# The heads loop of a gated delta rule: gate read from PSUM, a mask added by TensorE, partial sums left to TensorE, a product moved by a round, filling matmuls

## The reference, cut to what matters

```python
decay = jnp.exp(jnp.where(lower, g[..., :, None] - g[..., None, :], -jnp.inf))
L = jnp.where(strict, jnp.einsum('bhncd,bhnsd->bhncs', kb, k) * decay, 0.0)
T = lax.linalg.triangular_solve(eye + L, ...)
u = T @ vb
w = T @ (kb * jnp.exp(g)[..., None])
attn = jnp.einsum('bhncd,bhnsd->bhncs', q, k) * decay
...
    v_new = u_n - jnp.einsum('bhcd,bhde->bhce', w_n, state)
    o = q_n @ state + a_n @ v_new
...
zg = jax.nn.silu(z)
o = rmsnorm(o, norm_w) * zg
return o @ w_out
```

## Time and profile before

| | |
|---|---|
| runs | 1623.2 us median of 3 (1621.7 to 1625.29) |
| profiled execution | 1621.4 us, with a span of 1619.6 us |
| TensorE busy | 1554.8 us (96%) |
| VectorE, ScalarE, GpSimd busy | 1109.9, 932.7 and 493.4 us |
| granted TensorE clock, mean | 0.987 |
| heads loop, first p0 to last d5 | 196.3 to 327.1 us |

### The profile page before, as it was taken

How to read it: one execution, slowest core, us unless ns; L and a number is a source line. 1 busy time by engine, 2 the same in 40 slices (tenths; PEclk the granted TensorE clock), 3 DMA queues, 4 the chain that set the end, 5 groups by cost and what they waited for, 6 DMA issues and landing times.

```text
span 1619.6 us, 37025 instructions
## 1 busy us (share of the span) xinstructions
PE 1554.8 (96%) x13269; PEld 1429.3 (88%) x13269; DVE 1109.9 (69%) x2304; ACT 932.7 (58%) x1763; POOL 493.4 (30%) x405
## 2 busy tenths in 40 slices
PE   7899999899999999999999999999999999999998
PEld 6899877798998899888999999999999888888886
DVE  3787768656556653776478888798888555555554
ACT  1766567744555555545354444799898544555554
POOL 4000278661000040000067777766565100000000
PEclk9999979899999999999999999999999999999999
DMA  9668412454443344247455555544444666666663
GB/s 295 219 184 278 150 55 82 133 163 130 151 131 118 111 156 131 79 157 156 104 150 167 168 168 172 162 143 135 140 131 143 182 194 194 193 192 190 194 193 127
DMA packets 211832, 255.89 MB, mean 158 GB/s; under 512 B 15912, under 2 KB 193804, under 8 KB 211724
## 3 DMA queue, kind: packets, MB, share of 16 engines
q1 hardware_dynamic: 211723, 254.39, 53.2%
HBM read 253.29 MB, written 1.05 MB: 157 GB/s over the span
## 4 chain that ended last, share of the span: by engine, by line
PE 72%; DVE 11%; issue 5%; DMA 4%; ACT 4%; SPq 2%; DVEq 0%; ACTq 0%
PE ps L2253 22%; PE ps L2861 22%; PE ps L2843 10%; PE ps L2831 3%; DMA raw<-in_u_experts 3%; PE ps L2273 2%; PE ps L2551 2%; DVE raw L2014 2%; SPq L580 2%; PE ps L2628 1%; DVE w_lo L1396 1%; PE ps L2451 1%; DMA arena<-in_ada_w 1%; DVE arena L2067 1%; PE ps L2648 1%
## 5 line engine op out<-in xcount | busy, mean ns | idle before, releaser
L742 POOL TENSOR_TENSOR w_lo<-raw,w_hi 128x1024 fp32r<-128x1024 f32 x128 | 307.6, 2406 | 337.7 <-ACT w_hi L1265 337.6
L2253 PE MATMUL ps<-x_hi,w_hi 128*128 128x256 f32 x1088 | 315.3, 290 | 8.3 <-DVE w_lo L1396 3.0
L2253 PE MATMUL ps<-x_hi,w_lo 128*128 128x256 f32 x1088 | 308.2, 283 | 0.0
L2253 PE MATMUL ps<-x_lo,w_hi 128*128 128x256 f32 x1088 | 308.2, 283 | 0.0
L2212 DVE TENSOR_TENSOR w_lo<-raw,w_hi 128x1024 fp32r<-128x1024 f32 x124 | 152.0, 1226 | 143.2 <-ACT w_hi L1374 143.2
L1374 ACT ACTIVATE w_hi<-raw 128x1024 fp32r<-128x1024 f32 x124 | 131.6, 1061 | 168.0 <-PE ps L2861 168.0
L2253 PEld LDWEIGHTS ps<-x_hi,w_hi 128*128 128x128 f32 x1088 | 209.1, 192 | 15.3 <-issue 6.0
L2253 PEld LDWEIGHTS ps<-x_lo,w_hi 128*128 128x128 f32 x1088 | 209.2, 192 | 1.3 <-issue 1.2
L2253 PEld LDWEIGHTS ps<-x_hi,w_lo 128*128 128x128 f32 x1088 | 209.0, 192 | 0.0
L1265 ACT ACTIVATE w_hi<-raw 128x1024 fp32r<-128x1024 f32 x128 | 134.9, 1054 | 113.4 <-DVE raw L2014 113.2
L2806 PE MATMUL ps<-x_hi,w_hi 128*128 128x256 f32 x576 | 166.3, 289 | 10.6 <-ACT arena L1287 9.7
(11 more groups left out here) (446 smaller groups left out, 3563.7 us busy)
## 6 DMA issues: line engine op xcount, KB each, us to landing
raw<-in_u_experts SPq DMA_DIRECT2D x512, 128.0 KB, 2.7
raw<-in_v_experts SPq DMA_DIRECT2D x128, 512.0 KB, 4.3
arena<-in_ada_w SPq DMA_DIRECT2D x18, 1024.0 KB, 7.8
raw<-in_a_w_in SPq DMA_DIRECT2D x12, 1024.0 KB, 5.7
arena<-in_a_w_in SPq DMA_DIRECT2D x12, 1024.0 KB, 5.7
raw<-in_b_w_in SPq DMA_DIRECT2D x8, 1024.0 KB, 5.7
arena<-in_b_w_in SPq DMA_DIRECT2D x8, 1024.0 KB, 5.6
raw<-in_w_in SPq DMA_DIRECT2D x8, 1024.0 KB, 5.6
```

Source lines behind the costliest of these rows:

```text
L742: pool.tensor_tensor(UTL[e], UT[e % 2], UTH[e].bitcast(F32), ALU.subtract).then_inc(utl_ready, 1)
L2253: ins = mm(o[:, b * S:b * S + S], w[:, slot, kk, b * P:b * P + P], xx[:, (kk + turn) % KC, :], start=(kk == 0 and n == 0), stop=(kk == k - ...
```

## The change

- `decays` is gone from VectorE. A new `setup_masks` on TensorE adds `negu` (now bf16) to ROWS in PSUM, by two matmuls with a bf16 identity for each of two heads, after `betas` has read ROWS. `setup_decays` reads its exponent from PSUM, and `setup_values` waits for it.
- `finish_out` loses its copy to OS. A new `gated` on VectorE multiplies A2, read from PSUM, with the norm weight and the gate, into ZB, behind m4. F5 waits for it too, since it writes the same bank. `normed` is left with one instruction for each head.
- GpSimd leaves out the last of its 7 additions. `modulator` takes four matmuls in place of two, two for each of its 128-column halves, and stands behind F1 of the next round.
- `keep_wide` issues filling matmuls (bf16, 512 columns, result unused). A middle round has two in front of d0 and one in front of d4; rounds 0 and 7 have more.
- The orders change: `setup_keys` stands behind d1, F2 behind p2, `norm_sums` in front of p5, `betas` in front of c2, `lowers` behind m3, `setup_v` ahead of `spread`, and in round 7 the splits of ZB (L1405) one step earlier.

```diff
-                for half, done in ((4, 8), (2, 12), (1, 14)):
+                for half, done in ((4, 8), (2, 12)):
...
             def setup_decays(r):
+                if r.at:
+                    act.wait_ge(h_kd, r.count(2))
+                    act.wait_ge(h_at, r.count(2))
+                    act.wait_ge(h_lt, r.count(2))
                 for g in range(2):
                     act.wait_ge(h_dta, r.nth(g))
                     for cc in range(2):
-                        act.activation(two(DT[g])[:, cc, :], two(DT[g])[:, cc, :], ACT.Exp,
+                        act.activation(two(DT[g])[:, cc, :], ROWS[g][:, cc * 128:cc * 128 + 128], ACT.Exp,
...
-            def finish_out(r):
+            def finish_squares(r):
+                for g in range(2):
+                    act.wait_ge(h_o, r.nth(g))
+                    act.activation(SQo[g], A2[g], ACT.Square).then_inc(h_sq, 1)
...
                 if f:
-                    finish_out(f)
+                    finish_squares(f)
+                if n:
+                    setup_v(n)
                 spread(i, 0)
                 spread(i, 1)
-                if n:
-                    setup_v(n)
                 spread(i, 2)
...
-            def decays(r):
-                if r.at:
-                    v.wait_ge(h_kd, r.count(2))
-                    v.wait_ge(h_at, r.count(2))
-                for g in range(2):
-                    v.wait_ge(h_eg, r.nth(g))
-                    v.tensor_tensor(two(DT[g]), two(ROWS[g][:, 0:256]), bcast(negu, 2), ALU.add).then_inc(h_dta, 1)
...
-            def normed(r, g):
+            def gated(r):
+                if r.at >= 6:
+                    v.wait_ge(z_late, 1)
+                for g in range(2):
+                    v.wait_ge(h_sq, r.nth(g))
+                    zb = ZB[:, r.heads[g], :]
+                    v.scalar_tensor_tensor(zb, A2[g], COLS[:, CAN:CAN + 1], zb, ALU.mult, ALU.mult).then_inc(h_os, 1)
+
+            def normed(r, g):
                 v.wait_ge(h_orn, r.nth(g))
                 v.wait_ge(h_os, r.nth(g))
-                v.scalar_tensor_tensor(OS[g], OS[g], COLS[:, CAN:CAN + 1], RNo[g], ALU.mult, ALU.mult).then_inc(h_og, 1)
-                v.wait_ge(h_og, r.nth(g, 1, 1, 2))
                 zb = ZB[:, r.heads[g], :]
-                v.tensor_tensor(zb, OS[g], zb, ALU.mult).then_inc(h_out, 1)
+                v.tensor_tensor(zb, zb, RNo[g], ALU.mult).then_inc(h_out, 1)
...
-            def setup_values(r):
+            def setup_masks(r):
                 for g in range(2):
                     pe.wait_ge(h_eg, r.nth(g))
                     pe.wait_ge(h_xm, r.nth(g))
+                    for cc in range(2):
+                        ins = mm(ROWS[g][:, cc * 128:cc * 128 + 128], ident16, negu, start=False, stop=True, skip_group_check=True)
+                    ins.then_inc(h_dta, 1)
+
+            def setup_values(r):
+                for g in range(2):
+                    pe.wait_ge(h_dt, r.nth(g, 2))
...
                 for cc in range(2):
-                    ins = mm(MODP[:, cc:cc + 1], RAW[MOD_SLOT[r.side]][:, 0, cc * 128:cc * 128 + 128], ones[:, 0:1], start=True, stop=True)
+                    for half in range(2):
+                        ins = mm(MODP[:, cc:cc + 1], RAW[MOD_SLOT[r.side]][:, half, cc * 128:cc * 128 + 128], ones[:, 0:1],
+                                 start=(half == 0), stop=(half == 1))
...
+            def keep_wide(bank_, n):
+                for _ in range(n):
+                    mm(bank_[:, :], ident16, BG3, start=True, stop=True)
...
             def inner(i, f, n):
                 level_p(i, 0)
-                level_d(i, 0)
+                level_d(i, 0, 2)
                 if f:
                     finish(f, 0)
-                level_p(i, 1)
+                level_p(i, 1, 0 if f else 2)
                 if f:
                     finish(f, 1)
+                    modulator(f)
+                level_d(i, 1, 0 if f else 2)
                 if n:
                     setup_keys(n)
-                level_d(i, 1)
+                level_p(i, 2, 0 if n else 1)
                 if f:
                     finish(f, 2)
-                level_p(i, 2)
                 if n:
                     setup_rows(n)
-                level_d(i, 2)
+                level_d(i, 2, 0 if n else 1)
                 if f:
                     finish(f, 3)
+                if n:
+                    setup_masks(n)
                 level_p(i, 3)
                 if f:
                     finish(f, 4)
-                level_d(i, 3)
+                level_d(i, 3, 0 if f else 2)
                 if n:
                     setup_values(n)
-                level_p(i, 4)
-                level_d(i, 4)
+                level_p(i, 4, 0 if n else 2)
+                level_d(i, 4, 1)
                 if f:
                     finish(f, 5)
                 if n:
                     setup_low(n)
-                level_p(i, 5)
-                modulator(i)
                 if i.at + 2 < GQ:
                     norm_sums(Round(i.at + 2))
+                level_p(i, 5, 0 if f else 2)
                 level_d(i, 5)
...
             pe.wait_ge(cv_out, 16)
+            setup_masks(Round(0))
             setup_values(Round(0))
...
                 finish(Round(GQ - 1), step)
+                if step == 1:
+                    modulator(Round(GQ - 1))
```

More of the change, by code:

```diff
@@ L347, in program @@
         RNo = [temp(256)]
-        negu = temp(128)
+        negu = temp(64).bitcast(B16)
+        temp(64)
         strict = temp(128)
@@ L692, in _ @@
                                        ALU.mult).then_inc(mod_sum, 1)
-                for half, done in ((4, 8), (2, 12), (1, 14)):
+                for half, done in ((4, 8), (2, 12)):
                     pool.wait_ge(mod_sum, 15 * i + (24 + done))
                     for kk in range(half):
-                        pool.tensor_tensor(w[:, kk, :], w[:, kk, :], w[:, kk + half, :], ALU.add).then_inc(mod_sum, 1)
+                        pool.tensor_tensor(w[:, kk, :], w[:, kk, :], w[:, kk + half, :], ALU.add).then_inc(mod_sum, half if half == 2 and kk else 1)
                 if i + 1 < GQ:
@@ L1038, in _ @@
             finish_second(Round(GQ - 1))
-            finish_out(Round(GQ - 1))
+            finish_squares(Round(GQ - 1))
             finish_norms(Round(GQ - 1))
@@ L1631, in betas @@
                 for g in range(2):
+                    v.wait_ge(h_eg, r.nth(g))
                     v.tensor_tensor(two(KKb[g]), two(ROWS[g][:, 256:512]), KKs, ALU.mult).then_inc(h_xm, 1)
@@ L1703, in inner @@
                 close_level(i, 0)
+                mask_level(i, 1)
                 if ahead:
                     normalised_k(ahead)
-                mask_level(i, 1)
                 if f and f.at:
@@ L1709, in inner @@
                 close_level(i, 1)
+                if f:
+                    modulator(f)
                 if n:
@@ L1714, in inner @@
                     remainder(f)
-                close_level(i, 2)
                 if n:
-                    decays(n)
+                    betas(n)
                 else:
                     split_x_half(1, 0, ZB[:, 0:8, :])
+                close_level(i, 2)
                 mask_level(i, 3)
-                if n:
-                    betas(n)
-                close_level(i, 3)
-                mask_level(i, 4)
                 if n:
@@ L1728, in inner @@
                     split_x_half(1, 1, ZB[:, 0:8, :])
+                close_level(i, 3)
+                mask_level(i, 4)
+                if f:
+                    gated(f)
                 close_level(i, 4)
@@ L1747, in _ @@
             lo(T_AIN + 16, 0, 8)
-            decays(Round(0))
             betas(Round(0))
@@ L1758, in _ @@
             normed(Round(GQ - 2), 1)
+            modulator(Round(GQ - 1))
             remainder(Round(GQ - 1))
+            gated(Round(GQ - 1))
             for g in range(2):
@@ L2436, in level_p, with level_d @@
                 ins.then_inc(h_p, 1)
-            def level_d(r, j):
+            def level_d(r, j, spare=0):
+                if j == 0 and r.at:
+                    pe.wait_ge(h_xx, r.count(12))
+                keep_wide(PB, spare)
                 pe.wait_ge(h_pm, r.count(6, j + 1))
@@ L2493, in finish @@
                         pe.wait_ge(h_sq, r.nth(g))
+                        pe.wait_ge(h_os, r.nth(g))
                         mm(B2[g], ones, SQo[g], start=True, stop=True).then_inc(h_oss, 1)
@@ L2566, in _ @@
                 finish(Round(GQ - 1), step)
+                if step == 1:
+                    modulator(Round(GQ - 1))
             for u in range(1, 4):
                 pe.wait_ge(lo_ready, tile_no(T_AOUT, 0, u))
+                if u == 2:
+                    pe.wait_ge(ada_free, 10 + GQ)
                 if u < 3:
```

12 lines of the change are left out of this document (4 added, 8 removed).

## The result

The changed kernel took 1653.94 us (median of 4 runs, 1642.48 to 1656.62), the kernel before on the same chip 1623.91 us. The ratio is 1.0179, 95% interval 1.0158 to 1.0201. It is 30 us slower where I forecast 2.6, and lies outside my range. The profiled execution took 1656.09 us with a span of 1654.4, against 1621.4 and 1619.6.

What follows compares the result with a forecast made beforehand. It took the heads loop as the path: TensorE's throughput bounds a middle round's first half, VectorE works through the second. +1.6 + 6.6 - 0.3 - 5.0 - 0.3 + 0 = +2.6 on 1623.2 gave 1625.8 us, range 1614.5 to 1634.

Steps and rivals of the forecast that it cites:

- The keys, F2 and the rows only change places between the same neighbours.: First half of a middle round: reordering these on TensorE was given no cost.
- The first half, 10.5 us forecast: Middle round, d0 to end of p4, bound by TensorE's throughput: 9.36 plus 0.92 for `modulator` plus 0.25 for masks.
- Masks +0.25: First half of a middle round: four bf16 matmuls in `setup_masks` cost 0.25 us, bounds 0.2 and 1.2.
- The second half, 5.9 within 0.3: Middle round, end of p4 to next d0: VectorE loses 1.1 us, TensorE takes up the path, length stays 5.9 us.
- Six middle rounds, +6.6: Heads loop: each middle round 1.1 us longer, 16.4 us, six giving +6.6; bounds +0.8 and +1.8 each.
- Ahead of round 0, +1.6: Before the loop: the later mask and exponentials delay p0 of round 0 by 1.6 us, from 0.8 to 2.1.
- Rounds 0 and 1, the clock, -5.0: Fills and keys behind d1 keep the clock up in rounds 0 and 1, saving 5.0 us of 34.5.
- Round 7 and behind: Last round keeps its clock fall, net -0.3 us; output projection 0.
- The clock falls ahead of round 0: First rival: clock at 0.50 before d1 of round 0, the 5.0 not won, about 3 more paid; 1633.8 us, chance 0.26.
- VectorE the limit: Rival for middle rounds: VectorE, not TensorE, sets the period, so its savings come through; 1615.6 us, chance 0.20.
- The clock stays up everywhere: Rival: the clock stays up to the end, round 7 included, 2.6 us less; 1623.2 us, chance 0.20.
- granted clock 1.0 from 196 to 308: Sign for the forecast: full clock through the heads loop from its start, then a fall in round 7.

Runs made afterwards that it cites:

- a_copyfirst: The changed kernel with VectorE's copy of the modulation moved ahead of `close_level(i, 1)`; 1628.32 us, 1.0039 of the kernel before.
- a_gapfill: The changed kernel with three more filling matmuls behind d1 in rounds 1 to 7, where the keys wait; 1633.32 us, 1.0083 of the kernel before.
- a_mod2: The changed kernel with GpSimd's last addition back and two matmuls in `modulator` in place of four; 1636.99 us, 1.0076 of the kernel before.
- a_nofill: The changed kernel without any of its filling matmuls; 1648.54 us, 1.0181 of the kernel before.
- a_nsold: The changed kernel with `norm_sums` back behind p5; 1640.0 us, 1.0127 of the kernel before.
- b_modlate: The kernel before with only the two-matmul modulation product behind F1 of the next round, keys behind d1, copy behind c1; 1634.89 us, 1.0082 of the kernel before.
- a_modold: The changed kernel with the four-matmul modulation product and its copy back behind p5 and m5 of the same round; 1626.45 us, 1.0043 of the kernel before.
- b_masks: The kernel before with only the mask part: masks added by TensorE, no decays, `betas` ahead of c2, exponentials from PSUM; 1627.82 us, 1.0024 of the kernel before.
- b_edge: The kernel before with filling matmuls only in rounds 0, 6 and 7; 1619.13 us, 0.9975 of the kernel before.
- b_edge_again: Unaltered repeat of b_edge; 1618.02 us, 0.9967 of the kernel before.
- a_repaired: The changed kernel with the modulation copy ahead of c1, two matmuls in `modulator`, and `norm_sums` behind p5; 1628.41 us, 1.0038 of the kernel before.
- b_gate: The kernel before with only the gate part: `gated` from PSUM, no output copy, shorter `normed`, `lowers` ahead of c3; 1623.41 us, 0.9998 of the kernel before.

## Why the prediction was wrong, point by point

**"The keys, F2 and the rows only change places between the same neighbours."** This is the step that failed. The keys didn't just change places with d1: they came to stand one instruction behind the product whose copy they wait for. I asked which new waits the change adds, and looked for them among the added lines. The wait was an old one that had always been met. Measured: 0.86 us a round (a_copyfirst), and the clock. The sum also took the middle rounds at the full clock without a reason and gave their clock no case of its own. It fell in all six, which is 12.0 of the 27.7 us of the next point.

**Where the 27.7 us of rounds 1 to 6 are.** At the full clock a changed round takes 17.89 us (a_gapfill), so six of them cost 6 x 2.61 = 15.7. The falls cost the rest: 123.06 - 6 x 17.89 = 15.7 us, of which the kernel before had 95.39 - 6 x 15.28 = 3.7 for its fall in round 1 and a pause of 1.1 in round 3. Together 15.7 + 12.0 = 27.7.

**The first half, 10.5 us forecast.** It is 11.47, and 10.61 without the wait. `modulator` +0.92: the rows show 0.95 for the 8 records, and the half grew by 10.61 - 9.36 - 0.45 = 0.80. Right. The four passes of the second pair take 0.45 us (a_mod2), 0.11 us each. The rule of the Trainium skill that I set beside it (TensorE: Matmul & The Clock Gate, LDWEIGHTS) gives 107 ns for 128 columns, and the trace agrees closely. Masks +0.25: mis-sized, 0.43 to 0.45 in both kernels that isolate them, inside my bounds of 0.2 and 1.2. Four bf16 matmuls cost about 0.11 each, more than the 99 ns of a weight load and not half of it. The mask's wait for `betas` at nothing: right, no row shows it waiting.

**The second half, 5.9 within 0.3.** 6.41 us, outside the 0.3. The fills cost 0.36 (a_nofill), and `norm_sums` ahead of p5 0.35 (a_nsold, with the fills in). My schedule put the end of `norm_sums` and p5 at 3.8 us behind p4; it is 255.63 - 251.60 = 4.03, and c5, which I had ending at 5.3, ends at 5.8 (L1671, 257.00 + 0.42). The gate took 0.86 us for two, where I had 0.8, and gave back 0.11 a round. That the product "was free" at its old place holds in the old order only (b_modlate, without it there, has a second half of 5.98 for 5.92): in the new one it costs 0.46 there (a_modold).

**Six middle rounds, +6.6.** Even at the full clock it is +15.7, 2.61 a round where my upper bound was 1.8. The bounds were narrower than my own terms allowed. The masks alone could be 0.95 dearer (1.2 for 0.25), the second half 0.3 and the wait for `betas` 0.7; with the 1.1 of the sum that is up to 3.05, not 1.8. They also left no room for a term I didn't have. That 2.61 lies inside such wider bounds would have been luck, since its largest part, the wait of the keys, was in none of them.

**Ahead of round 0, +1.6.** +1.2 here and 2.1 in b_masks, within 0.8 to 2.1. Of the changed kernel the last mask, the values and p0 (timeline of TensorE):

```profile
193.87 0.40 PE L2396 MATMUL ps<-arena,small 128*128 128x128 bf16 x4
...
194.87 0.95 PE L2403 MATMUL ps<-small,arena 128*128 128x128 f32 x4 [0.61 <-ACT arena L942]
...
197.49 0.45 PE L2441 MATMUL ps<-arena 32*32 32x32 f32 x32 [0.84 <-DVE arena L1641]
```

The chain through the mask and the exponentials is the one I drew, and a little shorter. The size is not confirmed to better than a microsecond or two: two executions of b_edge, the same kernel, began the loop at 196.18 and 197.78, and variants of the changed kernel with the same instructions ahead of it at 197.49 to 200.53.

**Rounds 0 and 1, the clock, -5.0.** Failed in the changed kernel: the clock was down from 199 on, ahead of d1, as the first rival said, and down again in round 1 by the wait. The size of the term was right: b_edge_again gets 5.5 us from these two rounds, and a_nsold, a_copyfirst and a_repaired have a round 0 of 14.0 to 14.5, where I said about 14. Why the changed kernel's clock falls in round 0 and that of a_nsold, which has the same instructions there up to p5, does not, stays open.

**Round 7 and behind.** The fall in round 7 came, as forecast, with +1.3 for -0.3. In the output projection I had put nothing, and it is 2.7 us. The clock is down there for a while, where in the kernel before it was at 1.00 from 327.1 to 388.2 (a stretch of the changed kernel, after the loop's end):

```profile
357.50:372.00 14.50, 13.95 (x90) 13.84 (x90) 4.87 (x8) 3.85 (x10) 1.05 (x2) 0.76 0.38 118
```

The last product lies in this part; how much of the 2.7 is its own and how much the clock's wasn't separated.

**The rivals.** "The clock falls ahead of round 0" came true by its own mark, 0.50 before d1 of round 0, and these two rounds are 2.8 us longer in place of 5.0 shorter; its 1633.8 is far below the result since it held nothing of the middle rounds. "VectorE the limit": out; its busy time in a middle round fell from 13.04 to 11.83 us and the rounds got longer. "The clock stays up everywhere": out. No case had the clock fall in the middle rounds. The sign that I named for the forecast, "granted clock 1.0 from 196 to 308", is the one that showed it at a glance.

**The rule on the clock.** The Trainium skill, same page, Part 1, calls the lower clock the default, which activity releases. In this trace a busy engine was not enough: within 198 to 202 TensorE was busy 3.57 of 4 us, and the clock went down. The Trainium skill's section on HAM oscillation, on that page, has the clock go down in every pass of a loop because of a wait in every pass. This trace agrees in kind; the wait here is 0.84 us, and a_copyfirst and a_gapfill show that in the changed kernel it decides.

## What to carry to other kernels

When an instruction is moved, list the waits of everything that it passes and of everything that now follows it, the unchanged ones above all: for each, find the instruction that releases it, what that one stands behind on its own engine, and how far ahead it now is. Here one copy of 0.12 us behind `close_level` instead of ahead of it cost 1.40% of the 1.79% (a_copyfirst), 23 us of 29.

Where filling work stands matters more than how much there is. Here three fills a round in the gap gave 16 us, thirty-six elsewhere none. A gap closed by one repair can open again by the next, as in a_repaired, so the waits have to be read anew each time. Read the granted clock of every repeat of a loop before and after, not the busy share.

An operation that is free beside other work has a price elsewhere, and few moving columns don't make it small: here a pass with one moving column cost 0.11 to 0.12 us, more than a bf16 load of 128 columns of weights (99 ns).

## What the runs showed of the hardware

- In the changed kernel the clock fell in every middle round behind 0.95 us of one-column matmuls, 0.44 us of 32x32 blocks and 0.84 us of waiting, and in round 3 it stayed down for 6.9 us. Where a middle round's granted clock was 0.83 for 1.00, the round was 2.7 to 2.8 us longer (20.6 for 17.89, 20.3 for 17.53 in a_nofill); in a_mod2, at 0.70 for 1.00, 5.3.
- In the profiled executions with the gap filled by three 512-column matmuls (a_gapfill), or all but closed (a_copyfirst), it never fell in the middle rounds. With the product at half length it fell in two of six, with a wait of 1.3 us in the kernel before in one of six, and with the long product at its old place and no wait in two of six (a_modold). Other executions of a_copyfirst and b_modlate had a lower mean clock (0.983, 0.978) than the profiled ones (0.990, 0.987).
- TensorE stood still for 0.9 to 2.2 us in some rounds, mostly within a row of like matmuls, with no engine to wait for in the profile. The clock fell behind the pause of 2.18 us (b_edge, round 7) and that of 0.94 (b_gate, round 3), and stayed at 1.00 in the rounds with the pauses of 1.1 us (kernel before, round 3), 1.28 (a_gapfill, round 5) and 1.55 (a_repaired, round 6). Where the pauses come from no run shows.
